# Second layer's dilated attention: scores and turns between the halves of a query panel, two out-projection panels inside the last two slots

## What is computed

```python
h = x @ b_w_in                                   # 18 query heads of 128, and 4 memory queries of 64
mix = dilated_attention(qd, shared_k, shared_v)  # 6 slots, each with 3 groups of queries on one key/value head
# per slot and group: s = q @ k.T * 128**-0.5, masked by the group's window and dilation;
# the three groups share one softmax, their probabilities are added up; o = p @ v
mo = mem_attn(qm, mem_k, mem_v)                  # 4 heads
y = concatenate([mix, mo], -1) @ w_out           # 1024 x 1024
x = layer_norm(alpha * x + y)
```

## Time and profile before

| | |
|---|---|
| median of 3 runs | 2866.92 us (2864.12 to 2877.24) |
| the profiled execution | 2869.54 us |
| its span | 2867.7 us |
| its mean granted TensorE clock | 0.984 |
| TensorE busy | 2759.9 us, 96% of the span |
| VectorE busy | 1733.8 us, 60% |
| ScalarE busy | 1279.5 us, 45% |
| GpSimd busy | 135.7 us, 5% |

### The profile page before, as it was taken

The page is one execution under the profiler, slowest core; times in us unless marked ns, Lnnn a source line. Parts: engine busy times, 40 slices in busy tenths (PEclk is TensorE's granted clock), DMA queues, the critical chain, the costliest instruction groups (busy, mean ns, idle before and its releaser), DMA issues.

```text
span 2867.7 us, 45582 instructions
## 1 busy us (share of the span) xinstructions
PE 2759.9 (96%) x18636; PEld 2492.4 (87%) x18636; DVE 1733.8 (60%) x2778; ACT 1279.5 (45%) x1467; POOL 135.7 (5%) x68
## 2 busy tenths in 40 slices
PE   8999999899999999999999999988999999999997
PEld 7879888699886999999999888977999999999886
DVE  5646446365454699845555565556799745555565
ACT  4555344454353454444444444443554444444442
POOL 0000000000000510000000000000600000000000
PEclk9999999999997999999999999999999999999999
DMA  5215542155532445565656675413446756565672
GB/s 209 104 72 210 191 182 88 59 195 191 197 118 92 164 158 208 221 238 204 218 200 213 219 272 206 173 72 119 149 145 225 264 204 220 200 212 203 234 263 88
DMA packets 74409, 516.00 MB, mean 180 GB/s; under 512 B 8272, under 2 KB 8544, under 8 KB 18592
## 3 DMA queue, kind: packets, MB, share of 16 engines
q1 hardware_dynamic: 58576, 424.70, 41.3%
q0 software_dynamic: 10208, 43.45, 4.4%
q10 hardware_dynamic: 5488, 45.94, 4.0%
HBM read 474.22 MB, written 39.85 MB: 179 GB/s over the span
## 4 chain that ended last, share of the span: by engine, by line
PE 88%; DVE 9%; issue 1%; ACT 1%; DMA 1%; ACTq 0%; DVEq 0%
PE lin L1419 17%; PE lin L1420 17%; PE lin L1421 17%; PE m L1420 8%; PE m L1419 8%; PE m L1421 8%; PE m L1841 4%; PE lin L1590 1%; DVE lo L863 1%; PE m L1534 1%; PE m L1404 1%; PE m L1555 1%; PE m L1758 0%; PE m L1821 0%; PE m L1663 0%
## 5 line engine op out<-in xcount | busy, mean ns | idle before, releaser
L863 DVE TENSOR_TENSOR lo<-raw,hi 128x2048 fp32r<-128x2048 f32 x381 | 870.8, 2291 | 679.2 <-ACT hi L440 678.2
L440 ACT ACTIVATE hi<-raw 128x2048 fp32r<-128x2048 f32 x403 | 769.0, 1911 | 497.6 <-PE m L1421 346.8
L1419 PE MATMUL lin<-xh,hi 128*128 128x256 f32 x3376 | 974.7, 289 | 13.5 <-DVE lo L863 5.6
L1420 PE MATMUL lin<-xl,hi 128*128 128x256 f32 x3376 | 957.1, 284 | 0.0
L1421 PE MATMUL lin<-xh,lo 128*128 128x256 f32 x3376 | 956.8, 283 | 0.0
L1419 PEld LDWEIGHTS lin<-xh,hi 128*128 128x128 f32 x3376 | 647.0, 192 | 22.5 <-DVE lo L863 6.8
L1420 PEld LDWEIGHTS lin<-xl,hi 128*128 128x128 f32 x3376 | 647.5, 192 | 3.6 <-issue 1.0
L1421 PEld LDWEIGHTS lin<-xh,lo 128*128 128x128 f32 x3376 | 647.0, 192 | 0.0
L1420 PE MATMUL m<-lo,ah 128*128 128x512 f32 x1024 | 402.2, 393 | 0.0
L1419 PE MATMUL m<-hi,ah 128*128 128x512 f32 x1024 | 401.0, 392 | 0.0
L1421 PE MATMUL m<-hi,al 128*128 128x512 f32 x1024 | 399.4, 390 | 0.0
(11 more groups left out here) (328 smaller groups left out, 2722.5 us busy)
## 6 DMA issues: line engine op xcount, KB each, us to landing
raw<-stream SPq DMA_DIRECT2D x403, 1024.0 KB, 4.8
gate_table<-stg ACTq DMA_DIRECT2D x16, 2048.0 KB, 11.5
g<-gate_table POOLq DMA_DIRECT2D x32, 1024.0 KB, 8.3
rows<-rows ACTq DMA_DIRECT2D x4, 1024.0 KB, 6.8
memh<-mem_turned_scratch POOLq DMA_DIRECT2D x3, 1024.0 KB, 5.2
meml<-mem_turned_scratch POOLq DMA_DIRECT2D x3, 1024.0 KB, 8.7
x_scratch<-x ACTq DMA_DIRECT2D x2, 1024.0 KB, 4.3
x<-x_scratch ACTq DMA_DIRECT2D x2, 1024.0 KB, 6.1
```

The source lines that it names most:

```text
L440: act.activation(HI[i % SLOTS][:], RAW[:, i % SLOTS, :], ACT.Copy).then_inc(hi_ready, 1)
L863: dve.tensor_tensor(LO[i % SLOTS][:], RAW[:, i % SLOTS, :], HI[i % SLOTS][:].bitcast(F32), ALU.subtract).then_inc(lo_ready, 1)
L1419: pe.matmul(out_, ah, bh, start=first, stop=False, **kw)
L1420: pe.matmul(out_, ah, bl, start=False, stop=False, **kw)
```

## The change

Second layer only, save for the order of products inside `wide` and the signal of `mix_low`, which all callers share.

- Slots 0 to 3: TensorE does the first scores of the next slot, half of the query panel, the second scores, the turns, the other half of the panel, the values.
- Slots 4 and 5: the first two out-projection panels (rows 0 to 3 of the mix) run in four token halves (`out_half`) between scores, turns and values. They wait for the second `mix_low`. Only the last two panels stay in `wide` behind the slots. There the products go by row block in the order 2, 3, 0, 1 (before 0, 1, 2, 3), and the first of them waits for the low parts one by one. The warm-up products are gone in this layer.
- VectorE: weight remainders after n = 4, 6, 8, 10 and 11, one each; the low parts of rows 0 to 3 ahead of n = 9, the others behind the slots.
- ScalarE: the copy of a slot's turns now stands ahead of the exponential; the high parts of rows 0 to 2 and 3 in slot 3, of 6, 7 and 4 in slot 4, of 5 in slot 5; the high part of the fourth out-projection panel in slot 4.

```diff
@@ -686,28 +686,36 @@
                         if kt % 2 == 1:
                             a.mark(ins, sem("mix_high0"))
                 else:
-                    def slot_out(sl):
+                    def slot_turned(sl):
                         act.wait_ge(sem("dpt_done"), sl + 1)
                         a.mark(act.activation(flat(PTD[:]), M[2][:], ACT.Copy), sem("dpt_ready"))
+
+                    def slot_out(sl):
                         if p1 + sl < N_MIX2[l]:
                             mixing_panel(p1 + sl)
+                        if sl == SLOT_H - 3:
+                            act.wait_ge(sem("do_ready"), 3)
+                            mix_high(0, 3)
+                        elif sl == SLOT_H - 2:
+                            hi_to(s0 + N_MIX2[l] + N_OUT)
+                            mix_high(6, 8)
                         act.wait_ge(sem("dpv_done"), sl + 1)
                         a.mark(act.activation(MIX2[:, sl, :], M[3][:, 0:256], ACT.Copy), sem("do_ready"))
+                        if sl >= SLOT_H - 3:
+                            act.wait_ge(sem("do_ready"), sl + 1)
+                            mix_high(sl, sl + 1)
 
                     for n in range(2 * SLOT_H):
+                        if n >= 3 and n % 2 == 1:
+                            slot_turned(n // 2 - 1)
                         act.wait_ge(sem("dnb_ready"), n + 1)
                         c = 48 + 2 * (n % 2)
                         a.mark(act.activation(S3[:, n % 2, :], S3[:, n % 2, :], ACT.Exp, scale=KEYS ** -0.5, bias=SMALL[:, c:c + 1],
                                               accum_out=SMALL[:, c + 1:c + 2]), sem("dexp_ready"))
                         if n >= 3 and n % 2 == 1:
                             slot_out(n // 2 - 1)
-                    act.wait_ge(sem("do_ready"), SLOT_H - 1)
-                    mix_high(0, SLOT_H - 1)
-                    mix_high(6, 8)
+                    slot_turned(SLOT_H - 1)
                     slot_out(SLOT_H - 1)
-                    act.wait_ge(sem("do_ready"), SLOT_H)
-                    mix_high(SLOT_H - 1, SLOT_H)
-                    hi_to(s0 + N_MIX2[l] + 3)
                 w0 = s0 + N_MIX2[l] + N_OUT2[l]
                 hi_to(w0 + 3)
                 act.wait_ge(sem("ln_var"), 2 * l + 1)
@@ -1144,7 +1152,7 @@
 
                 def mix_low(a, b, n):
                     dve.wait_ge(sem(f"mix_high{l}"), n)
-                    v.mark(dve.tensor_tensor(flat(XL[:, a:b, :]), flat(MIX2[:, a:b, :]), flat(XH[:, a:b, :].bitcast(F32)), ALU.subtract))
+                    v.mark(dve.tensor_tensor(flat(XL[:, a:b, :]), flat(MIX2[:, a:b, :]), flat(XH[:, a:b, :].bitcast(F32)), ALU.subtract), sem(f"mix_low{l}"))
 
                 if l == 0:
                     lo_to(s0 + N_MIX2[l])
@@ -1200,12 +1208,17 @@
 
                     lo_to(s0 + 9)
                     slot_max(0)
+                    o = s0 + N_MIX2[l]
+                    weights = {4: o, 6: o + 1, 8: o + 2, 10: o + 3, 11: o + N_OUT}
                     for n in range(2 * SLOT_H):
-                        if n == 4:
-                            lo_to(s0 + N_MIX2[l])
+                        if n == 9:
+                            mix_low(0, 3, 1)
+                            mix_low(3, 4, 2)
                         if n + 1 < 2 * SLOT_H:
                             slot_max(n + 1)
                         slot_sum(n)
+                        if n in weights:
+                            lo_to(weights[n])
                 lo_to(s0 + N_MIX2[l] + 3)
                 if l == 0:
                     for kt in range(6):
@@ -1214,9 +1227,9 @@
                         v.mark(dve.scalar_tensor_tensor(out=XL[:, kt, :], in0=M[kt // 2][:, 256 * (kt % 2):256 * (kt % 2) + 256], scalar=P2[:, 4 + kt:5 + kt],
                                                         in1=XH[:, kt, :].bitcast(F32), op0=ALU.mult, op1=ALU.subtract))
                 else:
-                    mix_low(0, SLOT_H - 1, 1)
-                    mix_low(6, 8, 2)
-                    mix_low(SLOT_H - 1, SLOT_H, 3)
+                    mix_low(6, 8, 3)
+                    mix_low(4, 5, 4)
+                    mix_low(5, 6, 5)
                 dve.wait_ge(sem("dve_step"), v.count["dve_step"])
                 v.step(dve.memset(SMALL[:, 46:47], 0.0), sem("mix2l_ready"))
                 w0 = s0 + N_MIX2[l] + N_OUT2[l]
@@ -1459,7 +1472,7 @@
                 ins.then_inc(hp_used, 1)
                 between(1)
 
-            def wide(i, i0, n, hh, hl, k0, first, last):
+            def wide(i, i0, n, hh, hl, k0, first, last, low={}):
 
                 pe.wait_ge(lo_ready, i + 1)
                 wh, wl = (t[i % SLOTS][:].rearrange("p (k n) -> p k n", k=KT // 2) for t in (HI, LO))
@@ -1467,9 +1480,11 @@
                     j = i0 + 2 * n + tt
                     if first and reads_before(j) > 0:
                         pe.wait_ge(bank_free[j % 4], reads_before(j))
-                    for k in range(KT // 2):
+                    for k in (2, 3, 0, 1):
+                        if k in low and tt == 0:
+                            pe.wait_ge(sem("mix_low1"), low[k])
                         ins = three(PS[j % 4][:], hh[:, k0 + k, P * tt:P * tt + P], hl[:, k0 + k, P * tt:P * tt + P], wh[:, k, :], wl[:, k, :],
-                                    first and k == 0, last and k == KT // 2 - 1, skip_group_check=True)
+                                    first and k == 2, last and k == 1, skip_group_check=True)
                 ins.then_inc(hp_used, 1)
 
             def attention_pe(g0, heads, q, k, val, part, PM=PM, PT=PT, panel=lambda n: None):
@@ -1781,10 +1796,8 @@
 
                     slot_scores(0)
                     slot_scores(1)
-                    for sl in range(SLOT_H):
-                        if sl + 1 < SLOT_H:
-                            slot_scores(2 * sl + 2)
-                            slot_scores(2 * sl + 3)
+                    def slot_turns(sl):
+
                         pe.wait_ge(sem("dsm_ready"), 2 * sl + 2)
                         if sl >= 1:
                             pe.wait_ge(sem("dpt_ready"), sl)
@@ -1792,20 +1805,58 @@
                             for qt in range(2):
                                 ins = pe.transpose(M[2][:, 256 * kt + P * qt:256 * kt + P * qt + P], PD[:, sl % 2, qt, P * kt:P * kt + P], cst("ident"))
                         ins.then_inc(sem("dpt_done"), 1)
-                        if p1 + sl < N_MIX2[l]:
-                            mixing_panel(p1 + sl)
+
+                    def slot_values(sl):
+
                         pe.wait_ge(sem("dpt_ready"), sl + 1)
                         if sl >= 1:
                             pe.wait_ge(sem("do_ready"), sl)
                         for kt in range(2):
                             ins = pe.matmul(M[3][:, 0:256], VD[:, kt, P * sl:P * sl + P], PTD[:, kt, :], start=(kt == 0), stop=(kt == 1))
                         ins.then_inc(sem("dpv_done"), 1)
+
+                    def out_half(u, tt):
+
+                        o = s0 + N_MIX2[l]
+                        pe.wait_ge(sem("mix_low1"), 2)
+                        pe.wait_ge(lo_ready, o + u + 1)
+                        j = o + 2 * u + tt
+                        if reads_before(j) > 0:
+                            pe.wait_ge(bank_free[j % 4], reads_before(j))
+                        wh, wl = (t[(o + u) % SLOTS][:].rearrange("p (k n) -> p k n", k=KT // 2) for t in (HI, LO))
+                        for k in range(KT // 2):
+                            ins = three(PS[j % 4][:], XH[:, k, P * tt:P * tt + P], XL[:, k, P * tt:P * tt + P], wh[:, k, :], wl[:, k, :],
+                                        k == 0, False, skip_group_check=True)
+                        if tt == 1:
+                            ins.then_inc(hp_used, 1)
+
+                    for sl in range(SLOT_H - 2):
+                        slot_scores(2 * sl + 2)
+
+                        def second(c):
+                            if c == 0:
+                                slot_scores(2 * sl + 3)
+                                slot_turns(sl)
+
+                        half(s0 + p1 + sl, "cc", between=second)
+                        slot_values(sl)
+                    slot_scores(2 * SLOT_H - 2)
+                    out_half(0, 0)
+                    slot_scores(2 * SLOT_H - 1)
+                    slot_turns(SLOT_H - 2)
+                    out_half(0, 1)
+                    slot_values(SLOT_H - 2)
+                    out_half(1, 0)
+                    slot_turns(SLOT_H - 1)
+                    out_half(1, 1)
+                    slot_values(SLOT_H - 1)
                     pe.wait_ge(sem("do_ready"), SLOT_H)
                     pe.wait_ge(sem("dsc_read"), 2 * SLOT_H)
-                warm(7, M[3])
-                pe.wait_ge(sem("mix2l_ready"), l + 1)
-                for u in range(N_OUT):
-                    wide(s0 + N_MIX2[l] + u, s0 + N_MIX2[l], u % 2, XH, XL, 4 * (u // 2), u < 2, u >= 2)
+                if l == 0:
```

(4 more changed lines are left out.)

## The result

| | before | after |
|---|---|---|
| median | 2868.39 us (5 runs, 2864.12 to 2877.24) | 2849.18 us (5 runs, 2847.52 to 2850.64) |
| ratio | | 0.9927 (95% interval 0.9914 to 0.9939) |
| profiled span | 2867.7 us | 2845.7 us |
| the stage: first scores to end of the out-projection | 1888.09 to 1985.76, 97.67 us | 1886.03 to 1963.76, 77.73 us |

The change makes the kernel 0.7% faster. The forecast was 2847 us, and a stage of 77 to 78 us. The stage gained 19.9 us where 20.0 was forecast. The other 2.1 us of the difference of the two spans arose before the stage began.

A forecast was written before the change was run, and what follows sets the result against it. TensorE, holding 88% of the chain of waits, bounds the kernel. The stage would end at 1965.7 instead of 1985.7 us, 20.0 us less, giving 2849.5 us; the median lies 2.6 us lower, so 2847 us, range 2840 to 2857.

The forecast's parts named there:

- Slot 0: Second layer's first slot: turns still start at 1899.65, held by VectorE; slot 1 starts at 1904.0, not 1906.9.
- Slots 1 to 3, 10.0 us: Second layer: each slot takes 10.0 us instead of 12.30, with 9.9 and 10.2 as ends.
- the extra 0.1 us for splitting the panel: Slots 1 to 3: splitting a query panel adds one change of stream, so 9.89 us was taken as 10.0.
- the 7.27 us: Turns, panel and values of one slot on TensorE, kept in the new slot beside two scores of 1.31 us.
- Remainders, nothing: VectorE's weight remainders, one per slot, 2.29 us each, cost TensorE nothing.
- the cover: Slots 1 to 3: 0.4 us between VectorE's sum, done at 5.2, and TensorE asking for it at 5.6.
- The wait on ScalarE, 1.35 us twice: Before slots 3 and 4, TensorE waits for ScalarE's query panel eviction behind a high part; ends 0 and 1.9.
- Slots 4 and 5: Out-projection halves run between scores, turns and values; waits of 0.7 and 0.6 us; values and copy done at 1954.8.
- The end: Behind the slots two out-projection panels remain, 10.9 us, ending at 1965.7 against 1985.7; what follows moves as a block.
- The clock, 1.00 throughout: TensorE keeps the full clock in the stage, as the new order has waits of 1.4 us at most.
- Rivals: Remainders on the chain 2855.7 us, 9%; out-projection halves not in slots 4 and 5 2859.8 us, 7%; low clock, 4%.
- the third rival: In the stage the broken order brings the 1.2 GHz level; some 62 us of work low gives 2909 us; 4%.

The follow-up runs named there:

- the exponential-first kernel: The changed kernel with ScalarE's copy of the turns behind the exponential again, as before the change; stage 81.5 us, 3.7 more, in one execution.

## Why the prediction was right

- *Slot 0*: turns at 11.56 us into the stage before (1899.65 - 1888.09) and at 11.57 after. Right.
- *Slots 1 to 3, 10.0 us*: slot 1 took 9.62 us, and the kernel with ScalarE's eviction first, which has no waits there, 9.6, 9.8 and 9.8 us; all are below the lower end of 9.9. Two terms were too large. One is the extra 0.1 us for splitting the panel: in the chain the whole panel takes 5.74 us before (from the end of the turns, 1911.95 + 0.66, to the values at 1918.35), and the two halves take 2.87 us each. The other is in the 7.27 us, which was taken where the turns had waited: they take 0.66 us there, and 0.44 in slot 1, where they didn't. Together with rounding that made 0.2 to 0.4 us per slot too much. With the waits for ScalarE the first scores are 9.6, 11.4 and 11.5 us apart, where 10.0, 11.4 and 11.4 were forecast.
- *Remainders, nothing*: right in the sum to some 0.1 us. But behind n = 4 the cover was nothing and not 0.4 us: the sum that slot 2's turns need is done 5.31 us into the slot (forecast 5.2), and TensorE asks at 5.3 (forecast 5.6). With that remainder doubled, all of the added time came back. That the forecast held here was luck to a part.
- *The wait on ScalarE, 1.35 us twice*: 1.50 and 1.63. Right in place and cause: without the high part ahead of the eviction both are gone. It is longer because TensorE was earlier.
- *Slots 4 and 5*: waits of 0.7 and 0.6 us forecast, 0.43 and 0.53 measured; the third panel at 66.7 us into the stage, forecast 1954.8 - 1888.1 = 66.7. That this agrees to 0.1 us is luck to a part. The faster slots and the longer waits on ScalarE nearly cancelled (slot 4 at 48.35 us, forecast 1936.7 - 1888.1 = 48.6), and the rest went where VectorE's last sum decides: slot 5's turns start at 61.93, forecast 1950.1 - 1888.1 = 62.0.
- *The end*: 11.0 us for two panels, forecast 10.9. What follows is unchanged, as forecast.
- *The clock, 1.00 throughout*: right for this kernel. The reason given was too simple. The prediction read from the trace that it falls only where TensorE stands still longest, and left out that slot 0 before has a wait of 2.04 us, at a clock of 1.00 before and behind it. In the experiments it fell behind a wait of 2.23 us twice, did not behind one of 2.26 us, and did behind waits of 0.60 and 1.25 us. The Trainium skill, "TensorE: Matmul & The Clock Gate", section "A second HAM failure mode: psum-queue depth-cycling", says that frequent short pauses can do it. The exponential-first kernel agrees with that once (0.70 of full clock); the kernel with the doubled remainders doesn't: its waits of 0.99, 0.98, 1.32, 0.37, 1.28 and 2.26 us within 25 us are more and longer, and its clock stayed at 1.00. Neither the last wait nor the sum of the waits orders these cases. What decides stays open: each of them was seen once or twice.
- *Rivals*: the halves did run in slots 4 and 5; no product of the stage ran at the low level. The price of the third rival was real, though small: one fall costs 1 to 3.4 us here, not 62.

The median fell by 19.2 us (0.9927 of 2868.39 would be 20.9) where 20.0 was forecast.

## What to carry to other kernels

Where an engine waits for a chain that another engine runs, look for work behind the wait that needs nothing of the chain, and put it in halves ahead of each link; it costs nothing as long as the other engine's work per round stays under the new, shorter round, so sum that work up again with the new period. Then look at each in-order queue for what stands ahead of a result that the sped-up engine now asks for earlier: here a 1.8 us weight conversion ahead of a 0.6 us copy took back 3 us before slot 4. When a wait is only moved, look at the clock behind its new place before counting the gain.

## What the runs showed of the hardware

TensorE's granted clock is not told by the last wait alone: a 2.23 us wait was followed by some 3.4 us at the low level in two executions of the same kernel, a 2.26 us wait in another kernel, behind five others, was not, and waits of 0.6 us with two of 1.25 us were. Three warm-up products of 0.44 us, put into the 2.23 us, kept the clock at 1.00 in the one execution profiled, and shortened the stage by 1.6 us. A wait costs TensorE more than the idle time in its bracket, since products overlap where there is none: 0.86 us for 0.60, 0.82 for 0.47, and 1.6 for 1.50 (slot 2 with and without the wait for ScalarE). Splitting a panel costs nothing measurable (5.74 us whole, 2.87 us for each half).
